# A diffusion-transformer layer on eight cores: four score banks, three steps of lead, and merge weights converted ahead of their use

## What is computed

```python
def layer(x, mod, ...):
    sh_a, sc_a, g_a, sh_f, sc_f, g_f = jnp.split(mod, 6, axis=-1)   # mod = silu(c) @ w_mod + b_mod
    h = rms_norm(x, norm_a) * (1.0 + sc_a) + sh_a
    z = h @ w_in       # attn q | k | v | ret q | k | v | swish gate | gate A | gate R
    # A: attention, 16 heads of 128, 4 KV heads; q, k RMS-normed, 2-D rotary on sample tokens,
    #    a sample reads 512 cached keys besides its own 1024, a prompt its own 256
    # B: retention, 8 heads (key 128, value 256), both directions, chunks of 128
    o_r = groupnorm(o_r) * ret_norm * silu(g_r)
    merged = sigmoid(gate_a) * (o_a @ w_ba) + sigmoid(gate_r) * (o_r @ w_br)
    x = x + g_a * (merged @ w_out)
    h = rms_norm(x, norm_f) * (1.0 + sc_f) + sh_f
    x = x + g_f * ((silu(h @ w_g) * (h @ w_u)) @ w_d)               # D_FF = 5632
    return x            # a last rms_norm outside; new k, v and retention states are outputs too
```

## Time and profile before

| | |
|---|---|
| median of 3 runs | 3723.93 us (3713.81 to 3953.22) |
| profiled execution, its own time | 3722.31 us |
| span of the slowest core (core 1) in it | 3721.2 us |
| spans of the eight cores | 3685.6 to 3721.2 us |
| PE busy | 3377.6 us (91%) |
| DVE, ACT, POOL busy | 1116.0 (30%), 726.1 (20%), 219.7 us (6%) |
| HBM read, written | 902.53 MB, 41.98 MB |

### The profile page before, as it was taken

One profiled execution on the slowest core, in us unless ns is written; L12 is line 12 of the kernel. 1 busy time (PEld: TensorE's weight loads), 2 busy tenths in 40 slices (PEclk: granted clock), 3 DMA queues, 4 the chain that ended last, 5 costly groups with the idle time before them and its releaser, 6 DMA issues.

```text
span 3721.2 us, 52224 instructions; the slowest of 8 cores (3685.6 to 3721.2 us)
## 1 busy us (share of the span) xinstructions
PE 3377.6 (91%) x19697; PEld 1721.0 (46%) x19697; DVE 1116.0 (30%) x2685; ACT 726.1 (20%) x1454; POOL 219.7 (6%) x417
## 2 busy tenths in 40 slices
PE   2588888888999998989997998999999999999998
PEld 1244555664566553434443443444444444444443
DVE  1354454324666664112222113111112100120004
ACT  3222455642222220001111011110001000000001
POOL 0000000000000000000000000000000000000000
PEclk9798999999999999989998999999999999999999
DMA  9866544342232237989999996999899998999985
GB/s 201 164 125 108 93 91 96 61 86 43 55 69 60 49 70 154 188 162 202 181 170 189 194 162 147 201 169 167 146 151 213 168 173 147 149 223 169 173 146 129
DMA packets 99925, 525.29 MB, mean 141 GB/s; under 512 B 11808, under 2 KB 35296, under 8 KB 41056
## 3 DMA queue, kind: packets, MB, share of 16 engines
q0 software_dynamic: 61392, 422.60, 67.4%
q1 hardware_dynamic: 38288, 99.37, 8.3%
HBM read 902.53 MB, written 41.98 MB: 254 GB/s over the span
## 4 chain that ended last, share of the span: by engine, by line
PE 80%; DMA 11%; DVE 4%; issue 2%; ACT 2%; another core or an unknown queue 1%; DVEq 0%; SPq 0%; ACTq 0%; POOL 0%; POOLq 0%
PE pbk L296 78%; DMA sb_wsl<-w_mod 3%; DMA sb_xsl<-x 2%; DMA sb_wsl<-w_in 2%; DMA sb_wsl<-w_g 1%; PE pbk L299 1%; DMA sb_wsl<-w_u 1%; DMA sb_wsl<-w_br 1%; ACT sb_pT L303 1%; DVE sb_nw L314 1%; DMA sb_wsl<-w_out 1%; DMA sb_oaB<-oas 0%; DVE sb_ont L311 0%; DVE sb_ut L314 0%
## 5 line engine op out<-in xcount | busy, mean ns | idle before, releaser
L296 PE MATMUL pbk<-sb_hT,sb_wsl 128*128 128x512 bf16 x7296 | 1609.3, 381 | 32.6 <-DMA sb_wsl<-w_g 17.0
L296 PEld LDWEIGHTS pbk<-sb_hT,sb_wsl 128*128 128x128 bf16 x7296 | 715.2, 98 | 889.0 <-issue 60.2
L296 PE MATMUL pbk<-sb_wsl,sb_hT 128*128 128x256 bf16 (+1 forms) x2688 | 482.5, 329 | 25.7 <-ACT sb_hT L303 10.2
L296 PE MATMUL pbk<-sb_wsl,sb_hid 128*128 128x512 bf16 x2112 | 456.6, 379 | 1.5 <-DMA sb_wsl<-w_d 1.5
L296 PEld LDWEIGHTS pbk<-sb_wsl,sb_hT 128*128 128x128 bf16 x2688 | 259.8, 100 | 160.7 <-issue 59.5
L314 DVE TENSOR_TENSOR sb_hid<-pbk,sb_su 128x512 bf16<-128x512 f32 x132 | 91.1, 692 | 797.0 <-PE pbk L296 797.0
L296 PEld LDWEIGHTS pbk<-sb_wsl,sb_hid 128*128 128x128 bf16 x2112 | 206.5, 98 | 251.1 <-issue 2.4
L303 ACT ACTIVATE sb_pT<-pbk 128x512 bf16<-128x512 f32 x416 | 224.9, 603 | 114.9 <-PE pbk L296 113.7
L303 ACT ACTIVATE sb_su<-pbk 128x512 bf16<-128x512 f32 x132 | 78.8, 597 | 792.8 <-PE pbk L296 792.8
L314 DVE TENSOR_TENSOR sb_tB<-pbk,sb_bcg 128x512 f32<-128x512 f32 x96 | 66.2, 689 | 484.9 <-PE pbk L296 484.9
L296 PE MATMUL pbk<-sb_or,sb_wsl 128*128 128x512 bf16 x768 | 173.9, 385 | 31.6 <-DMA sb_or<-ors 27.0
(11 more groups left out here) (140 smaller groups left out, 2052.2 us busy)
## 6 DMA issues: line engine op xcount, KB each, us to landing
sb_wsl<-w_in POOLq DMA_DIRECT2D x84, 1024.0 KB, 13.5
sb_wsl<-w_g POOLq DMA_DIRECT2D x66, 1024.0 KB, 23.0
sb_wsl<-w_u POOLq DMA_DIRECT2D x66, 1024.0 KB, 22.9
sb_wsl<-w_d POOLq DMA_DIRECT2D x60, 1024.0 KB, 9.7
sb_wsl<-w_mod POOLq DMA_DIRECT2D x48, 1024.0 KB, 10.7
sb_wsl<-w_ba POOLq DMA_DIRECT2D x24, 1024.0 KB, 14.6
sb_wsl<-w_br POOLq DMA_DIRECT2D x24, 1024.0 KB, 13.9
sb_wsl<-w_out POOLq DMA_DIRECT2D x24, 1024.0 KB, 12.2
```

The lines of the kernel that those rows point to most:

```text
L296: K.op("pe", lambda: nc.tensor.matmul(out, lhsT=lhsT, rhs=rhs, start=start, stop=stop), reads, writes)
```

## The change

- A new HBM tensor `wc` holds the 40 merge tiles in bf16. `precast(2)` issues two conversions (fp32 tile in HBM to bf16 tile in HBM, on POOL's queue) behind each weight load of the retention: 44 places for 40 conversions, none left by head 7's V weights. The merge then loads its 120 tiles from `wc` (`mload`), each waiting for its conversion.
- `wadd` moves the rotation on by one, so the new slot is the last in turn.
- The scores use four banks (0, 1, 2, 5) and are issued three steps ahead of the exponential; projections, transposes and modulation steps of the attention share banks 6 and 7 in place of 5 to 7.
- One step of `kg` follows each V tile; `kg`'s last steps stand between V tiles 8 to 11, and `kg2` runs behind them. The copies of V out of PSUM are all on ACT.
- The modulation steps of `q0` use slots 4, 7 and 8 in turn.
- In merge block 0 gate R of column group 1 comes before the first attention branch.

```diff
...
     x1s_d = nc.dram_tensor("x1s", [NTOK, D], F32, kind="Internal").ap()
+    wc_d = nc.dram_tensor("wc", [40, 128, 4096], BF16, kind="Internal").ap()
...
-        def wload(parts, s=None):
+        def wload(parts, s=None, reads=()):
             if s is None:
...
                 ne = src.shape[1]
-                DMA("pool", wsl[s][:, off:off + ne], src, wsem[s], [], [wbuf[s]])
+                DMA("pool", wsl[s][:, off:off + ne], src, wsem[s], list(reads), [wbuf[s]])
             return wsl[s], wbuf[s]
+
+
+        mkeys = [k_ for cg in range(8) for k_ in (("w_in", win_idx(9216 + 256 * cg)), ("w_in", win_idx(11264 + 256 * cg)), ("w_ba", cg), ("w_br", cg))]
+        mkeys += [("w_out", i) for i in range(8)]
+        mcb = {k_: Buf() for k_ in mkeys}
+        mcsem, mcrot = [K.dsem(f"mc{i}") for i in range(8)], [Buf() for _ in range(8)]
+        mcn = [0]
+
+        def precast(n=1):
+            for _ in range(n):
+                i = mcn[0]
+                if i < len(mkeys):
+                    mcn[0] += 1
+                    DMA("pool", wc_d[i, :, :], wt(*mkeys[i]), mcsem[i % 8], [], [mcb[mkeys[i]], mcrot[i % 8]])
+
+        def mload(nm, i):
+            return wload([(wc_d[mkeys.index((nm, i)), :, :], 0)], None, [mcb[(nm, i)]])
...
             wlist.insert(wrot[0], len(wsl) - 1)
+            wrot[0] = (wrot[0] + 1) % len(wlist)
...
-        def proj_gen(pair, tiles, tab, tabb, ni, dstT, dstTb, banks, kout=False, pre=0, mods=(), step=4):
+        def proj_gen(pair, tiles, tab, tabb, ni, dstT, dstTb, banks, kout=False, pre=0, mods=(), step=4, mslots=(4,)):
...
                 if t in mods and len(modq):
-                    mod_step(pool_bank(banks), 4)
+                    mod_step(pool_bank(banks), mslots[len(modq) % len(mslots)])
                     yield 0.8
...
             src = bk[:].rearrange("p (g d) -> p g d", g=4)
-            if t % 2 == 0 or t >= 8:
-                CPA(vall[:, t, :, 0:128], src, [bkb], [vb[t]])
-            else:
-                CPV(vall[:, t, :, 0:128], src, [bkb], [vb[t]])
+            CPA(vall[:, t, :, 0:128], src, [bkb], [vb[t]])
             if t >= 8:
                 u, ub = nvst[t % 4], nvb[t % 4]
-                CPV(u[:], bk[:], [bkb], [ub])
+                CPA(u[:], bk[:], [bkb], [ub])
                 DMA("sp", nv_d[(t - 8) * 128:(t - 7) * 128, :], u[:], utsem[t % 4], [ub], [], is_out=True)
...
-        kdone = False
         for t in range(8):
-            for _ in range(3):
-                if not kdone and next(kg, "done") == "done":
-                    kdone = True
             v_tile(t)
+            next(kg)
             if t == 1:
...
                     modulate_p(k)
-        if not kdone:
-            run(kg)
         mod_step(pool_bank(ALLB), 4)
...
         for t in range(8, 12):
-            next(kg2, None)
             v_tile(t)
+            next(kg, None)
+        run(kg)
         run(kg2)
...
-        q0 = proj_gen(q0pair, range(NT), qtab, qtabb, 0, qT[0], qTb[0], ALLB, mods=(1, 3, 5, 7, 9, 11), step=16)
+        q0 = proj_gen(q0pair, range(NT), qtab, qtabb, 0, qT[0], qTb[0], ALLB, mods=(1, 3, 5, 7, 9, 11), step=16, mslots=(4, 7, 8))
         for n_, _ in enumerate(q0):
...
+            def sbank(ix):
+                i = (0, 1, 2, 5)[ix % 4]
+                return pbk[i], pbb[i]
+
             def emit_score(ix):
...
                 qt, qtb = qT[g % 2], qTb[g % 2]
-                bk, bkb = pbk[ix % 3], pbb[ix % 3]
+                bk, bkb = sbank(ix)
                 if kind == "S":
...
                 def out():
-                    tb_, tbb = pool_bank([5, 6, 7])
+                    tb_, tbb = pool_bank([6, 7])
                     tpv = tb_[:].bitcast(BF16)
...
-            emit_score(0)
-            emit_score(1)
+            for i in range(3):
+                emit_score(i)
             ix = 0
...
                 for e in range(ne):
-                    if ix + 2 < len(steps):
-                        emit_score(ix + 2)
-                    ACT(pT[slot_of[ix]][:], pbk[ix % 3][:], AF.Exp, [pbb[ix % 3]], [pTb[slot_of[ix]]], scale=ATT_SCALE)
+                    if ix + 3 < len(steps):
+                        emit_score(ix + 3)
+                    ACT(pT[slot_of[ix]][:], sbank(ix)[0][:], AF.Exp, [sbank(ix)[1]], [pTb[slot_of[ix]]], scale=ATT_SCALE)
                     pop(-(-nmm[0] // (ne - e)))
...
             slot2, wb2 = wload([(wt("w_in", win_idx(5120 + 256 * h)), 0)], s)
+            if s is None:
+                precast(2)
             wv = wview(slot2, 0, 16, 256)
...
             for h in range(2):
-                for x in v_gen(h, 2 + h, [5, 6, 7], 8):
+                for x in v_gen(h, 2 + h, [6, 7], 8):
                     yield x
                 if len(modq):
-                    mod_step(pool_bank([5, 6, 7]), 4)
+                    mod_step(pool_bank([6, 7]), 4)
                     yield 0.8
...
             if g < 3:
-                fill = proj_gen(qpairs[g + 1], range(NT), qtab, qtabb, 0, qT[(g + 1) % 2], qTb[(g + 1) % 2], [5, 6, 7],
+                fill = proj_gen(qpairs[g + 1], range(NT), qtab, qtabb, 0, qT[(g + 1) % 2], qTb[(g + 1) % 2], [6, 7],
                                 mods=(0, 1, 3, 5, 6, 8, 10), step=4)
...
             slot1, wb1 = wload([(wt("w_in", win_idx(3072 + 256 * h)), 0)])
+            precast(2)
             wqk = wview(slot1, 0, 16, 256)
...
             slot3, wb3 = wload([(wt("w_in", win_idx(7168 + 256 * h)), 0)])
+            precast(2)
             wgv = wview(slot3, 0, 16, 256)
...
+        assert mcn[0] == len(mkeys)
+
...
         def gate(b, cg, base, dst, dstb):
-            slot, wb = wload([(wt("w_in", win_idx(base + 256 * cg)), 0)])
+            slot, wb = mload("w_in", win_idx(base + 256 * cg))
             wv = wview(slot, 0, 16, 256)
...
         def branch(b, cg, nm, ai):
-            slot, wb = wload([(wt(nm, cg), 0)])
+            slot, wb = mload(nm, cg)
             wv = wview(slot, 0, 16, 256)
...
             if late:
-                order[0:9] = [("a", 0), ("r", 0), ("ba", 0), ("a", 1), ("r", 1), ("ba", 1), ("a", 2), ("br", 0), ("br", 1)]
+                order[0:9] = [("a", 0), ("r", 0), ("r", 1), ("ba", 0), ("a", 1), ("ba", 1), ("a", 2), ("br", 0), ("br", 1)]
             for kind, cg in order:
...
                 ns = slice(n * 512, (n + 1) * 512)
-                ws = wpair("w_out", 2 * n, None)
+                ws = []
+                for i in range(2):
+                    sl, wb = mload("w_out", 2 * n + i)
+                    ws.append((wview(sl, 0, 8, 512), wb))
                 for t in range(4):
...
                     acc(bk, bkb, 512, lambda k: mT[:, k, t * 128:(t + 1) * 128], lambda k: ws[k // 8][0][:, k % 8, :], 16,
```

## The result

The changed kernel takes 3756.74 us (median; 3717.84 for the kernel before, run beside it): a ratio of 1.0099, interval 1.0084 to 1.0114. The forecast was 3618. Some executions of every kernel run with one die at a lower clock and take longer; ratios and intervals leave them out, medians don't. In the changed kernel the V tiles of token tiles 4 and 5 take PSUM banks whose K tiles have not been read yet, so K of these two token tiles is made from V's values; the instructions are as many and of the same sizes. It is so as well in the experiments e1_pad, e2_noconv and e8_late, which keep its order of K and V.

The account below looks back on a forecast made before the run. PE was taken as the bound everywhere, so a change could only give back its waits. Terms 19 + 18 + 25 + 10 + 12 + 0 + 16 + 2 + 2 = 104 us off the profiled 3722.31 gave 3618 us, range 3597 to 3640.

Parts of the forecast that it names:

- What the conversions cost: Retention: 40 conversions at 6.2 us, 248 us of engine time against 414 free; cost put at nothing.
- The second rival: Retention: conversions over 10.3 us each no longer fit and stop it; at 15 us, 3808 us in total; chance 0.05.
- The prediction's last sign of being wrong: Whole kernel: the forecast would be wrong altogether if another core had a wait that core 1 lacks.
- One more step of lead is 0.44 us of PE work ... so most of it goes: Attention: waits for exponentials, 33.8 us, shrink to 8 with three steps of lead; gain 26 us.
- a loss of 24 for the two banks: Attention: projections left with two banks stall 38 us against 14 counted for three; loss 24 us.
- Rival A: Attention: the two banks cost more than counted, 24 us more, 3642 us in total; chance 0.12.
- K and V order: Before the attention: fewer stalls for scaled K tiles, 5 us, less 3 for bare last K tiles; net gain 2.
- The slot's turn at the FFN: First FFN tiles: new slot last in turn, three tiles loaded at the start; gain 18 us of 23.2.
- Merge and `w_out`: Merge and output projection: 19 for the slot, 25 and 12 for retention and attention outputs, 10 for `w_br` and `w_in`.
- The DMA share of 0.5 to 0.6: Merge: sign expected in the changed profile, the DMA share falling from 0.92 to 0.5 to 0.6.
- The third rival: Merge: a plain load takes as long as a converting one, share stays near 0.9, 3658 us; chance 0.12.
- The first stage: Up to the first score: 16 us from three modulation slots in the first q projection, 2 from token order; gain 18.

Follow-up runs that it names:

- e1_pad: The changed kernel with each row of `wc` padded by 256 bytes so that rows don't join: 3653.94 us, ratio 0.9825 to the kernel before.
- e2_noconv: The changed kernel with no conversions, the merge converting the original weights while loading: 3715.02 us, ratio 0.9982 to the kernel before.
- e8_late: The changed kernel, unpadded, with no conversions issued before retention head 1's second weight load: 3707.05 us, ratio 0.9986 to the kernel before.
- e10: e7 with the rows of the converted copy not padded: 3690.12 us, ratio 0.9921 to the kernel before.
- e7: The kernel before plus padded conversions, new slot last in turn, modulation slots, merge order and scores one step ahead: 3623.81 us, ratio 0.9743.
- e3: The kernel before with the change's attention alone (four score banks, three steps of lead, projections in two banks): 3736.55 us, single run, no ratio.
- e4: The kernel before with only the new slot put last in turn: 3688.14 us, ratio 0.9929.
- e12: The kernel before with padded conversions and their loads in the merge and output projection alone: 3673.32 us, ratio 0.9907.
- e11: e9 with the first nine steps of the merge's second half in the order of the kernel before: 3593.46 us, ratio 0.9692 to the kernel before.
- e9: e7 with the padded conversions issued later, none before retention head 1's second load: 3591.3 us, ratio 0.969 to the kernel before.

## Why the prediction was wrong

On core 1, stage against stage, the forecast of -104 us misses e1_pad's -70 by 34, and 27 of these are the attention. The changed kernel misses it by another 59 on core 1 and 101 on core 2, on core 1 nearly all in the attention's end and the retention (57), on core 2 for 89, with 7 more before the first score.

**The step that failed first: "What the conversions cost ... I cost it at nothing".** The bytes did fit: 10.3 us each were free and a conversion takes 9.2, though the sum had it at 6.2, so that the DMA share of the retention came out at 0.88 (core 2) and not at the 0.7 it named. Its reading of the loads was right, for no PE wait for `w_in` came up in the retention. But it asked only whether the bytes fit, and whose next load stands behind them on POOL. The second rival asked the same with another price. Neither asked who else uses the 16 engines: SP's state stores, state loads and head sums, in buffers that come round every 60 us or less. The prediction's last sign of being wrong did come up: the slowest core is now core 2, which waits 34.4 us for `S` and 20.8 for `osb` where core 1 waits 18.6 and 7.3. The runs show: with a packet of 0.9 us (e1_pad) the slowest store lands in 59 to 62 us and PE's long waits are gone; with one of 4.6 us in 75 to 82, and costs 100 us of the run (e1_pad against after, e10 against e7 66 us). The second rival's side of the result came true, its mechanism didn't.

**The step that failed second: "One more step of lead is 0.44 us of PE work ... so most of it goes".** The lead was the wrong quantity. The bank that a score needs is set by banks less lead, and both rose by one: the 33.8 us stayed 33.7 (gain 0, not 26). The other half, a loss of 24 for the two banks, came out at +22 by luck: it was counted as stall, but the waits for `t`, `ut` and `modt` are 22 us where 30 to 40 were forecast and 9.3 stood before, and PE's idle time grew by only 12 in e3. The rest is work at a lower clock, for which the prediction had no term here. Rival A, which had the two banks cost more than counted, names the right stage for another reason.

**K and V order.** Forecast 2 us. The prediction followed V tiles 4 and 5 into banks 4 and 5 "ahead of the evictions of the K tiles there" and concluded that the order holds no wait. It holds none because those K tiles are overwritten before they are read, as the section on the result says; the step was an error in the kernel and not a gain. e7_pad_lead1, which keeps the old order and has the new modulation slots, takes 312.8 us to the first score, e1_pad with both 313.6 (means of the cores). No run changes the order alone, and the kernels with the first stage of before differ by 5 us among themselves (319.3 to 324.8), so 2 us couldn't be seen.

**What held.** The slot's turn at the FFN: 18 forecast, 14.8 to 16 measured (after, e4). Merge and `w_out`: 66 forecast, 65.7 less the 6.9 us of the moved gate. (Of its terms the 19 for the slot was not seen alone beside full DMA engines: in e4 the wait for `or` grew by 18 in its place. Beside light loads it is some 14, e12 against e11.) The DMA share of 0.5 to 0.6: 0.51. The third rival is out: 119 plain loads took 38.5% of 935 us for 123.9 MB of q0, 3.0 us each, half of the converting ones. The Trainium skill's page DMA: Bandwidth & Descriptors, section Measured (HBM to SBUF, 128 partitions, SWDGE), has 6.15 us for 1 MB, which would have made them equal; the measurement decides. The first stage looks right on core 1, 16 to 17 us of 18, but that is luck in the choice of core: in the means of the cores the changed kernel gains 7 us, and the runs with three slots take 312.8 to 317.7 us against 319.3 to 324.8 with one.

## What to carry to other kernels

Before moving a transfer into a stage "with free DMA time", list every small transfer in that stage and the time until its buffer is used again; set against that time the turns it has to wait, each as long as one packet of the newcomer. Judge by the slowest landing, not by the median. Look at the packet count of a new kind of DMA: if it is far under that of its neighbours, make the rows not contiguous. For a rotation of banks count the distance back to the reader (banks less lead), not the distance ahead.

## What the runs showed of the hardware

- A DRAM to DRAM copy from float32 to bfloat16, both sides contiguous, 1 MB written: 32 packets of 32 KB, 4.6 us each, 9.2 us of all 16 engines. With a gap of 256 bytes behind each row of 8 KB: packets of 8 KB, 128 a conversion, 1.0 us each, and about the same in total: in e9, 850 to 1310 us, 6605 such packets, which are 51.6 transfers of loads and conversions together, took 411 us of all engines, 8.0 us each; with 15 loads at 6.2 and 3 at 3.0 taken off, 9.2 are left for a conversion.
- 128 KB on SP's queue land in 3 us beside converting loads and in 18 to 51 us (medians by core), at most 75 to 82, beside these copies; in 59 to 62 at most beside padded ones.
- Beside padded conversions the converting weight loads themselves land later, 26.9 us in place of 12.6. Why was not looked into; PE waited for none of them.
- After a wait PE ran slow. Eight matmuls of 256 columns on core 2 before and after one (clock granted from 799 to 806 us: 0.52, the lower level of 1.2 GHz; before the wait 1.00):

```profile
786.27 1.04 PE L297 MATMUL pbk<-sb_wsl,sb_hT 128*128 128x256 bf16 x8
...
799.77 1.87 PE L297 MATMUL pbk<-sb_wsl,sb_hT 128*128 128x256 bf16 x8 [10.47 <-DVE sb_oS L321]
```

  Over the retention of core 2 PE's idle time grew by 58 us against core 1 of before, the stage by 75; less the moved gate, some 10 us are this slower work.
